# Three lower splits given to GpSimd around the second attention, and two instructions put earlier in their queues

## The reference, cut to what matters

```python
def mla_attention(h, w_in, q_norm_g, kv_norm_g, w_uq, w_ukv, w_o, cos, sin):
    proj = h @ w_in                                   # 1024 -> 384 + 256 + 32
    c_q = rms_norm(proj[..., :384], q_norm_g)
    c_kv = rms_norm(proj[..., 384:640], kv_norm_g)
    k_pe = apply_rope(proj[..., 640:], cos, sin)      # one for all 16 heads
    q = (c_q @ w_uq).reshape(b, s, 16, 96)            # nope 64, rope 32
    kv = (c_kv @ w_ukv).reshape(b, s, 16, 128)        # k_nope 64, v 64
    ...  # scores per head, masked softmax, p @ v
    return o.reshape(b, s, 1024) @ w_o
```

## Time and profile before

| | us |
|---|---|
| median of 3 runs | 1020.29 (1019.63 to 1021.06) |
| the profiled execution, device time | 1021.66 |
| its span in the profile | 1019.8 |
| PE busy | 1003.1 (98%) |
| DVE busy | 760.3 (75%) |
| ACT busy | 573.4 (56%) |
| POOL busy | 6.6 (1%) |

### The profile page before, as it was taken

How to read it: one execution, slowest core, us unless ns; L and a number is a source line. 1 busy time by engine, 2 the same in 40 slices (tenths; PEclk the granted TensorE clock), 3 DMA queues, 4 the chain that set the end, 5 groups by cost and what they waited for, 6 DMA issues and landing times.

```text
span 1019.8 us, 18671 instructions
## 1 busy us (share of the span) xinstructions
PE 1003.1 (98%) x7220; PEld 932.5 (91%) x7220; DVE 760.3 (75%) x1017; ACT 573.4 (56%) x820; POOL 6.6 (1%) x20
## 2 busy tenths in 40 slices
PE   7999999999999999999999999999999999999997
PEld 6999999999999999977899999999998898888886
DVE  7576655557766656787778877778877888888886
ACT  6543454445544445657866555555646675666665
POOL 0000000000000000000000000000020000000000
PEclk9999999999999999999999999999999999999999
DMA  8645566556665564354464666674324574766651
GB/s 300 211 147 184 184 204 199 171 165 200 199 206 180 191 205 181 128 204 128 167 198 124 189 185 185 186 211 143 125 63 104 166 223 136 216 191 192 191 158 76
DMA packets 191265, 178.87 MB, mean 175 GB/s; under 512 B 17444, under 2 KB 169586, under 8 KB 191218
## 3 DMA queue, kind: packets, MB, share of 16 engines
q1 hardware_dynamic: 191074, 177.96, 56.5%
q10 hardware_dynamic: 144, 0.26, 0.1%
HBM read 177.15 MB, written 1.05 MB: 175 GB/s over the span
## 4 chain that ended last, share of the span: by engine, by line
PE 88%; DVE 5%; ACT 3%; DMA 2%; issue 1%; SPq 0%; DVEq 0%; ACTq 0%
PE psum L623 17%; PE psum L625 17%; PE psum L624 17%; PE psum L825 13%; PE psum L827 7%; PE psum L630 4%; PE psum L632 4%; PE psum L631 4%; DVE whl L1763 2%; ACT whl L1267 1%; DMA raw<-da_w_qkv 1%; DMA raw<-mla_w_o 1%; PE psum L973 1%; PE psum L957 1%; DMA x_rows<-x 1%
## 5 line engine op out<-in xcount | busy, mean ns | idle before, releaser
L1763 DVE TENSOR_TENSOR whl<-raw,whl 128x2048 fp32r<-128x2048 f32 (+2 forms) x145 | 298.2, 2061 | 79.0 <-ACT whl L1267 78.4
L1267 ACT ACTIVATE whl<-raw 128x2048 fp32r<-128x2048 f32 (+2 forms) x145 | 248.3, 1716 | 77.5 <-DMA raw<-w_ff 29.1
L623 PE MATMUL psum<-hT,whl 128*128 128x256 f32 (+1 forms) x784 | 219.9, 280 | 1.0 <-DVE hT L1838 1.0
L624 PE MATMUL psum<-hT,whl 128*128 128x256 f32 (+1 forms) x784 | 218.9, 279 | 0.0
L625 PE MATMUL psum<-hT,whl 128*128 128x256 f32 (+1 forms) x784 | 218.9, 279 | 0.0
L825 PE MATMUL psum<-hT,whl 128*128 128x512 f32 x608 | 213.0, 391 | 0.1
L827 PE MATMUL psum<-hT,whl 128*128 128x256 f32 x608 | 171.4, 282 | 0.0
L623 PEld LDWEIGHTS psum<-hT,whl 128*128 128x128 f32 (+1 forms) x784 | 147.1, 188 | 1.5 <-issue 0.7
L624 PEld LDWEIGHTS psum<-hT,whl 128*128 128x128 f32 (+1 forms) x784 | 147.2, 188 | 0.1
L625 PEld LDWEIGHTS psum<-hT,whl 128*128 128x128 f32 (+1 forms) x784 | 147.1, 188 | 0.0
L623 PE MATMUL psum<-lat,whl 128*128 128x256 f32 (+1 forms) x512 | 144.1, 281 | 0.3 <-DVE whl L1763 0.3
(11 more groups left out here) (258 smaller groups left out, 1583.0 us busy)
## 6 DMA issues: line engine op xcount, KB each, us to landing
raw<-w_ff SPq DMA_DIRECT2D x32, 1024.0 KB, 5.6
raw<-w_in SPq DMA_DIRECT2D x24, 1024.0 KB, 5.1
raw<-ffn_w_up SPq DMA_DIRECT2D x44, 512.0 KB, 5.1
q_sb<-ffn_w_up SPq DMA_DIRECT2D x44, 512.0 KB, 5.1
raw<-da_w_qkv SPq DMA_DIRECT2D x12, 1024.0 KB, 5.2
q_sb<-ffn_w_down SPq DMA_DIRECT2D x22, 512.0 KB, 3.8
raw<-ffn_w_down SPq DMA_DIRECT2D x22, 512.0 KB, 3.8
raw<-w_proj_a SPq DMA_DIRECT2D x4, 1024.0 KB, 5.2
```

Source lines behind the costliest of these rows:

```text
L623: mm(dst, weight(n, 0, cols, kt, c0, m), hi, start=start, stop=False, skip_group_check=True)
L624: mm(dst, weight(n, 0, cols, kt, c0, m), lo, start=False, stop=False, skip_group_check=True)
L1267: fn(whl[:, slot, 0, 0:w], landing(n)[:, 0:w], ACT.Copy).then_inc(hi_ready, 1)
L1763: tt(whl[:, slot, 1, 0:w], landing(n)[:, 0:w], whl[:, slot, 0, 0:w].bitcast(F32), ALU.subtract).then_inc(lo_ready, 1)
```

## The change

Four edits:

- ACT takes the first turned columns of the first attention before it splits chunk 76, and not behind that.
- POOL subtracts the lower halves of chunk 133, ahead of its copies, and of chunks 145 and 146 behind them. DVE does these three no more. Each POOL split waits for the high half and for the count of all lower splits before it, which DVE or POOL itself makes.
- DVE waits for the count of chunk 133 before its split of chunk 134, and for that of chunk 146 before its split of chunk 147, so that the count stays in order.
- At step c = 1, DVE splits chunk 140 between the two queries, and not behind the second.

```diff
@@ ACT, entry of the first attention
             take_rows(0, 0)
             take_rows(0, 1)
+            take_columns(0, 0)
             split_hi(n + 2)
-            take_columns(0, 0)
             take_columns(0, 1)
@@ POOL
+            def split_lo(n):
+                pool.wait_ge(hi_ready, n + 1)
+                pool.wait_ge(lo_ready, n)
+                w = chunk_words(n)
+                nc.gpsimd.tensor_tensor(whl[:, n % RING, 1, 0:w], landing(n)[:, 0:w], whl[:, n % RING, 0, 0:w].bitcast(F32),
+                                        ALU.subtract).then_inc(lo_ready, 1)
+
+            split_lo(N_MLA + 1)
             pool.wait_ge(kpe_ready, 1)
             ...
             ins.then_inc(kpe_spread, 1)
+            split_lo(N_WO2)
+            split_lo(N_WO2 + 1)
@@ DVE, end of a gated FFN
                     split_lo(n0 + 2 * units)
-                    split_lo(n0 + 2 * units + 1)
@@ DVE, second attention
+            dve.wait_ge(lo_ready, N_MLA + 2)
             split_lo(N_MLA + LEAD)
             ...
                 if c == 1:
                     next_query(1)
+                    split_lo(N_UQ + 1 + LEAD)
                 ...
                 if c < 7:
                     next_query(c + 1)
-                if c < 8:
+                if 1 < c < 6:
                     split_lo(N_UQ + c + LEAD)
             normalise_pair(7)
+            dve.wait_ge(lo_ready, N_WO2 + 2)
             split_lo(N_WO2 + LEAD)
```

## The result

| | us |
|---|---|
| changed kernel, median of 4 executions | 1030.57 (1028.78 to 1031.21) |
| before, median of 4 | 1020.25 (1019.63 to 1021.06) |
| ratio | 1.0098 (95% interval 1.008 to 1.0115) |
| profiled execution of the changed kernel | 1030.9, span 1029.1 |

The change costs 10.3 us. The forecast was 1020.5 with a range up to 1023.8. L957 are the transposes that wait for the normalisation, L623 is the projection that waits for `hT`.

What follows compares the result with a forecast made beforehand. PE, busy 98% of the span, was taken as the bound, so only its pauses count. Terms -0.7 + 1.0 - 0.3 + 0.2 = +0.2 us on the median gave 1020.5 us, range 1018.7 to 1023.8.

Steps and rivals of the forecast that it cites:

- Part 1: First attention: ACT takes the turned columns before its split, so PE's 0.67 us wait goes; -0.7 us.
- The price of a POOL split: Time of one POOL subtraction: taken as 4.4 us, between 2.3 and 6.9 us.
- The port and part 2: Second attention's entry: POOL's split of chunk 133 shuts out DVE's `rest_x` until 722.6; +1.0 us.
- Part 3: Loop step c = 1: chunk 140 split between the queries lets the normalisation end earlier; -0.3 us.
- Part 4: Loop's end: POOL splits chunks 145 and 146, DVE's normalisation goes first, the delay mostly covered; +0.2 us.
- Rival A: Loop's end: POOL gets in before the normalisation and shuts DVE out; +3.0 us, 1023.3 us, 27%.
- Rivals B and C: B: a POOL split takes 5.6 us, 1022.8 us, 9%; C: the port costs nothing, 1018.6 to 1019.0 us, 14%.

Runs made afterwards that it cites:

- e1: Changed kernel with chunks 145 and 146 split on DVE again, chunk 133 still on POOL; 1021.36 us.
- e3: Kernel before with the two order edits alone (columns earlier, chunk 140 between the queries), no split on POOL; 1020.18 us.
- e9: Changed kernel with 9 and 6 extra matmuls, results unread, on PE ahead of the transposes that wait for the blocked normalisations; 1028.88 us.
- e2: Changed kernel with chunk 133 split on DVE again; median 1028.66 us, seven executions at 1026.67 to 1030.41, three at 1020.1 to 1021.27.
- e5: Changed kernel with chunk 146 split on DVE again, 133 and 145 still on POOL; 1026.19 us, one execution of eight 1021.17.
- e6: Changed kernel with 18 and 11 extra matmuls, results unread, on PE ahead of the transposes that wait for the blocked normalisations; 1032.81 us.
- e8: Changed kernel with each POOL split made in four pieces of 512 words, one after the other; 1023.44 us.
- e4: Changed kernel with POOL waiting for DVE's normalisation of pair 4 before chunk 145 and of pair 5 before chunk 146; 1022.47 us.

## Why the prediction was wrong, step by step

- **Part 1, the columns (-0.7).** Right where it stands: -0.8 at the turn. Wrong as a term of the sum: 0.55 us are given back at the first pair. I asked only what was next on PE at that place, not which engine sets the next meeting, which here was DVE.
- **The price of a POOL split (4.4 us, 2.3 to 6.9).** 4.52 to 4.59 us in the sixteen instructions of all traces that run undisturbed. The Trainium skill's 4497 ns ("GPSIMD Engine Reference", "3.1 Elementwise — side-by-side cycle accounting") is closer than my middle of two bounds.
- **The port and part 2 (+1.0).** Right: POOL 718.12 to 722.71, `rest_x` shut out until then, +0.9 us at PE; e1 against e3 has 1.2.
- **Part 3 (-0.3).** Right: -0.4, and PE's longer wait for the normalisation as described.
- **Part 4 (+0.2) is the step that failed**, at the words "In the forecast DVE is first, and POOL gets in at 792.95". DVE was first in all six traces that have this collision: by 0.08 us in the changed kernel and e9, 0.09 in e2, 0.31 in e5, 0.03 in e6 and e8. That I had guessed well and not read: by the earlier trace rows the high half was done 0.05 us before DVE's start, and DVE was first only because POOL starts 0.08 us behind ACT's end (792.40 and 792.48). It did not help, because being first protects one instruction and `normalise_pair` is two. Where I had +0.2 us, the loop's end cost 9.2. I had read from the 3.26 us of the earlier trace rows that a run of instructions without a gap is not broken into. That row shows one of two outcomes; six of the thirteen traces have the other, 1.16 to 1.19 us. By this reading DVE is safe only when POOL arrives after its second operation has begun, 0.34 us behind the first. The 3 of 10 and 1 of 8 short executions of e2 and e5 fit that, but none of them was traced.
- **Rival A (+3.0, 27%)** has the mechanism that came, DVE shut out by POOL, at its place and with its first price (+4.0 us at the transposes), though by another order: POOL did not get in before the normalisation but in the middle of it. (Its own terms, added to 797.4, give 803.0 and not 803.3.) Its total was a third of the measured 10.3 us, for two reasons. I followed the delay through PE only, and not through ACT to POOL's second start, which put a second collision where none had been (4.4 us by e5, its part of the clock included). And I left out PE's clock, which fell to half behind both pauses (1.9 us net by the traces of e9 and the changed kernel, 1.7 by the medians).
- **Rivals B and C** did not come. The chances failed with the forecast: an order to be decided within 0.05 us, with a bad side of 4 us and more losses behind it, got 27%, and the range ended at 1023.8.

Adding up what was measured, each against its own before: 9.9 us at the loop's end (e1), 1.2 at the entry (e1 against e3), and -0.8 for the order edits (e3), together 10.3. What stays open is what decides between the two groups of e2. That it is when ACT's high half of chunk 145, and with it the DMA, is done fits the 0.34 us window. In the trace of e5, where POOL came latest, ACT had waited 0.35 us for this DMA, and 0.18 us in e4; in those of the changed kernel and e2 it had not waited. But no short execution was traced.

## What to carry to other kernels

Before work goes to GpSimd, list what VectorE does with two SBUF inputs in the same stretch, and count on each such instruction that comes up beside it having to wait for a whole GpSimd instruction, even in the middle of a pair. If the order matters, make it with a semaphore (8.1 us here) or cut the instruction up. A wait that hangs on two engines being ready within a few tenths is not a forecast but two, and the time of the worse one needs its own chain, through all engines and up to the next meeting. Where PE has been busy throughout, add the clock that can fall with a pause to its price, as it did with those of 2.5 and 3.9 us here.

## What the runs showed of the hardware

- DVE operations with two SBUF inputs and POOL operations excluded one another per instruction, not per run of instructions. Of two such DVE operations back to back the second took 5.02 us beside a POOL split of one instruction, 1.79 us beside one in quarters (e8), and 0.68 undisturbed. The Trainium skill, "SBUF — State Buffer", section "SBUF: two separate sides", has the exclusive hold for a whole instruction, and every trace here agrees.
- A DVE operation with one input in PSUM ran beside a POOL split at its normal 0.69 us (e4, from 793.92).
- A POOL subtraction of 128x2048 took 4.52 to 4.59 us undisturbed, DVE's 2.28.
- A waiting DVE split got in between POOL's sixteen copies in six traces (1.16 to 1.19 us, the copies together 7.11) and not in seven (3.24 to 3.29 us and 6.38). The instructions around it are the same in all thirteen kernels.
- Behind waits of PE of 3.9 us and of 2.5 us in otherwise full work, the clock was granted at half for 3.4 us each time. In e5 it was at half for 6.8 us around a wait of 3.9 us. In e9, with PE kept at work but for 1.2 us, it stayed at 1.00.
